# The last expert pair's down product by column halves, and residual rows added by TensorE, in a two-layer hybrid trunk

## What is computed

```
def reference(x, ...):
    h = layer_norm(x, ln_in_g, ln_in_b)
    for l in range(DEPTH):                        # DEPTH = 2
        mix = hybrid_mixer(h, w_in[l], ...)       # begins with p = h @ w_in
        h = layer_norm(DEEPNORM_ALPHA * h + mix, ln_mix_g[l], ln_mix_b[l])
        ffn = grouped_moe(h, w_router, router_bias, w_gate[l], w_up[l], w_down[l])
        h = layer_norm(DEEPNORM_ALPHA * h + ffn, ln_ffn_g[l], ln_ffn_b[l])
    return h

def grouped_moe(h, ...):
    ...
    for e in range(N_EXPERTS):                    # 16
        y = (silu(hf @ w_gate[e]) * (hf @ w_up[e])) @ w_down[e]
        out = out + gates[:, e:e + 1] * y
```

## Time and profile before

| | us |
|---|---|
| median of 3 runs | 691.44 |
| lowest and highest of the 3 | 691.26, 691.76 |
| the profiled execution, whole | 691.46 |
| its span, first to last instruction | 689.6 |
| TensorE busy in the span | 658.3 (95%) |
| VectorE busy | 321.0 (47%) |
| last pair's down, layer 0 | 332.87 to 339.96 |
| last pair's down, layer 1 | 667.82 to 674.91 |

### The profile page before, as it was taken

How to read it: one execution, slowest core, us unless ns; L and a number is a source line. 1 busy time by engine, 2 the same in 40 slices (tenths; PEclk the granted TensorE clock), 3 DMA queues, 4 the chain that set the end, 5 groups by cost and what they waited for, 6 DMA issues and landing times.

```text
span 689.6 us, 7631 instructions
## 1 busy us (share of the span) xinstructions
PE 658.3 (95%) x3105; PEld 339.1 (49%) x3105; DVE 321.0 (47%) x614; ACT 166.7 (24%) x324; POOL 71.2 (10%) x67
## 2 busy tenths in 40 slices
PE   8989999999999999998989999989999999999992
PEld 5854587543333553332478557855333436333331
DVE  6898877610321312320589978682220330320327
ACT  3511753231110221101153138424101114101100
POOL 3503100420000000000070040006000000000001
PEclk9999999999999999999999999999999999999997
DMA  8999936099999999999999973335999999999991
GB/s 286 366 390 414 387 124 244 1 360 397 428 431 428 426 429 427 429 423 419 401 382 395 419 314 123 122 123 208 363 420 428 431 426 429 426 428 429 416 407 66
DMA packets 39580, 240.70 MB, mean 349 GB/s; under 512 B 4524, under 2 KB 8948, under 8 KB 24180
## 3 DMA queue, kind: packets, MB, share of 16 engines
q1 hardware_dynamic: 36756, 236.49, 84.4%
q10 hardware_dynamic: 2784, 3.67, 1.5%
HBM read 239.10 MB, written 1.05 MB: 348 GB/s over the span
## 4 chain that ended last, share of the span: by engine, by line
PE 73%; DVE 11%; DMA 10%; ACT 2%; SPq 1%; issue 1%; POOL 0%; DVEq 0%; POOLq 0%; ACTq 0%
PE bank L591 22%; PE bank L624 10%; DMA ring<-in_w_up 8%; PE bank L495 8%; PE bank L509 6%; PE bank L569 5%; PE bank L606 5%; PE bank L660 4%; PE bank L639 4%; DVE mix L1470 4%; PE bank L707 2%; DMA ring<-in_w_in 2%; DVE in_lo L1236 2%; PE bank L614 1%; PE bank L779 1%
## 5 line engine op out<-in xcount | busy, mean ns | idle before, releaser
L591 PE MATMUL bank<-ring,xe 128*64 128x512 f32 x768 | 167.4, 593 | 0.0
L1397 DVE TENSOR_TENSOR area_b<-area_b,bank 128x512 f32<-128x512 f32 x16 | 11.0, 688 | 230.7 <-PE bank L591 166.6
L591 PEld LDWEIGHTS bank<-ring,xe 128*64 128x64 f32 x768 | 54.8, 137 | 108.3 <-issue 107.8
L624 PE MATMUL bank<-ring,area_b 128*64 128x512 f32 x384 | 85.0, 595 | 0.0
L1417 DVE SCALAR_TENSOR_TENSOR y_lo<-bank,slot_gate,y_hi 128x512 fp32r<-128x512 f32 x32 | 24.0, 750 | 87.7 <-ACT y_hi L984 87.7
L1085 POOL TENSOR_TENSOR rstd<-var_eps,half_neg 128x1 f32<-128x1 f32 x18 | 11.8, 661 | 510.1 <-DVE var_eps L1184 510.1
L606 PE MATMUL bank<-ring,xe 128*64 128x512 f32 x256 | 57.0, 595 | 3.4 <-DMA ring<-in_w_up 2.6
L495 PE MATMUL bank<-ring,xT_area 128*128 128x512 f32 x128 | 55.9, 592 | 0.0
L624 PEld LDWEIGHTS bank<-ring,area_b 128*64 128x64 f32 x384 | 26.5, 137 | 50.0 <-issue 50.0
L1470 DVE SCALAR_TENSOR_TENSOR mix<-mix,tapsT 128x256 f32<-128x256 f32 x120 | 49.8, 476 | 0.0
L984 ACT ACTIVATE y_hi<-bank,slot_gate 128x512 fp32r<-128x512 f32 x32 | 22.0, 687 | 98.4 <-PE bank L624 70.7
(11 more groups left out here) (173 smaller groups left out, 857.7 us busy)
## 6 DMA issues: line engine op xcount, KB each, us to landing
ring<-in_w_gate SPq DMA_DIRECT2D x32, 2048.0 KB, 19.9
ring<-in_w_up SPq DMA_DIRECT2D x32, 2048.0 KB, 20.6
ring<-in_w_down SPq DMA_DIRECT2D x32, 2048.0 KB, 20.7
ring<-in_w_in SPq DMA_DIRECT2D x9, 2048.0 KB, 17.9
ring<-in_w_out SPq DMA_DIRECT2D x4, 2048.0 KB, 20.2
ring<-in_w_in SPq DMA_DIRECT2D x2, 1024.0 KB, 7.7
h<-in_x SPq DMA_DIRECT2D x2, 512.0 KB, 4.0
ln_par<-in_ln_mix_g ACTq DMA_DIRECT2D x2, 512.0 KB, 17.0
```

The source lines that it names most:

```text
L591: mm = pe.matmul(bank[2 + m][e * SLOTS:(e + 1) * SLOTS, :], xe[:, k, at + e * SLOTS:at + (e + 1) * SLOTS], w[e][:, k * DE:(k + 1) * DE], s ...
L624: mm = pe.matmul(bank[5 + n][e * SLOTS:(e + 1) * SLOTS, :], hidT[:, k, e * SLOTS:(e + 1) * SLOTS], w[e][:, k * D + n * BANK:k * D + (n + 1 ...
```

## The change

Five edits.

1. In the last pair of each layer, down goes by column halves: all of half 0 (k = 0 to 3), then half 1. It waits for unit 4 and unit 5 at its beginning, and frees unit 4 after k = 1 of half 1. combine parts 0 and 1 stand inside half 1, ahead of k = 2.
2. add_rows: after down, TensorE multiplies the second half of the residual rows with the identity into bank[2] and bank[3], one fp32 matmul of 128x512 for each block, and combine parts 2 and 3 accumulate on it. VectorE's add_back of parts 2 and 3 is gone in this pair. The statistics of these parts are taken from PSUM, and so is the input of the normalisation, which is now two instructions of 512 columns for each block.
3. VectorE takes add_back 0, 1 and sum_stats 0, 1 between y_lo of half 0 and y_lo of half 1.
4. turn_input transposes half 0 of block 0, half 0 of block 1, half 1 of block 0, half 1 of block 1. ScalarE scales the eight chunks of block 0, VectorE the eight of block 1, and the first slab's products go through the chunks 0 to 7 and wait for both engines at each.
5. KEEP_TURN is 10 where it was 18.

The branch for an expert with more than 64 tokens gets two copies ahead and two behind; with these inputs it isn't entered (the trace has one pass of 8 pairs for each layer).

```diff
-KEEP_START, KEEP_MIX, KEEP_ROUTER, KEEP_SLOTS, KEEP_TURN = 18, 6, 18, 6, 18
+KEEP_START, KEEP_MIX, KEEP_ROUTER, KEEP_SLOTS, KEEP_TURN = 18, 6, 18, 6, 10
...
+            def turn_input(l):
+                for half in range(2):
+                    for b in range(TB):
+                        pe.wait_ge(norm_ready, 2 * TB * l + b + 1)
+                        for c in range(4):
+                            mm = pe.transpose(bank[2 * b + half][:, c * P:(c + 1) * P], normal[:, b, 4 * half + c::KC], ident)
+                        mm.then_inc(tr_pe, 1)
...
+                    if ps.main and j == pairs - 1:
+                        w = [landed_unit(PAIR_UNITS * j + 4 + u).rearrange("p (e c n) -> p e c n", e=2, c=2)
+                             for u in range(2)]
+                        for n in range(2):
+                            for k in range(FC):
+                                if n and k == 2:
+                                    combine(j, (0, 1))
+                                for e in range(2):
+                                    mm = pe.matmul(bank[5 + n][e * SLOTS:(e + 1) * SLOTS, :],
+                                                   hidT[:, k, e * SLOTS:(e + 1) * SLOTS],
+                                                   w[k // 2][:, e, k % 2, n * BANK:(n + 1) * BANK],
+                                                   start=k == 0, stop=k == FC - 1)
+                                if n and k % 2:
+                                    mm.then_inc(ps.used, 1)
+                            if n == 0:
+                                mm.then_inc(s["down_half"], 1)
+                        return
...
+                def add_rows(j):
+                    added(j - 1, 4)
+                    for b in range(TB):
+                        pe.matmul(bank[LAST_COMB_BANKS[2 + b]][:, :], ident, acc[:, b, BANK:D], start=True, stop=False)
...
-                combine(pairs - 1, range(4))
+                if ps.main:
+                    add_rows(pairs - 1)
+                    combine(pairs - 1, (2, 3))
+                else:
+                    combine(pairs - 1, range(4))
...
-                        c = n // 2 + 4 * (n % 2)
+                    for c in range(KC):
                         if k == 2:
-                            pe.wait_ge((tr_act, tr_dve)[n % 2], TR * l + 4 * (TB - 1) + n // 2 + 1)
+                            pe.wait_ge(tr_act, TR * l + c + 1)
+                            pe.wait_ge(tr_dve, TR * l + c + 1)
...
                         if ps.main and j == pairs - 1 and n == 0:
-                            add_back(j, (0,))
+                            add_back(j, (0, 1))
+                            sum_stats(j, (0, 1))
                 if ps.main:
-                    add_back(pairs - 1, (1,))
-                    sum_stats(pairs - 1, (0,))
-                    add_back(pairs - 1, (2,))
-                    sum_stats(pairs - 1, (1, 2))
-                    add_back(pairs - 1, (3,))
-                    sum_stats(pairs - 1, (3,))
+                    for b in range(TB):
+                        nth("comb", pairs - 1, 3 + b, 4)
+                        dve.bn_stats(stats[:, b, 1, :], bank[LAST_COMB_BANKS[2 + b]][:, :]).then_inc(s["stats"], 1)
...
-                        norm_center(norm[b], acc[:, b, :], b)
+                        dve.wait_ge(ln_rstd, norm[b] + 1)
+                        for n in range(2):
+                            ins = dve.tensor_scalar(normal[:, b, n * BANK:(n + 1) * BANK], rows[b][n], mv[:, b, 0:1],
+                                                    rstd[:, norm[b]:norm[b] + 1], ALU.subtract, ALU.mult)
+                        ins.then_inc(norm_ready, 1)
```

More of the change, by code:

```diff
@@ L655, in combine @@
                         if banks[k] == COMB_BANKS[k] and k >= 2:
-                            nth("added", j, k - 1, 4)
+                            added(j, k - 1)
                         elif k < 2 and j:
-                            nth("added", j - 1, k + 3, 4)
+                            added(j - 1, k + 3)
+                        rows_in_bank = ps.main and j == pairs - 1 and n == 1
                         for part in (y_hi, y_lo):
                             mm = pe.matmul(bank[banks[k]][:, :], back[:, b, :], part[:, n * BANK:(n + 1) * BANK],
-                                           start=part is y_hi, stop=part is y_lo)
+                                           start=part is y_hi and not rows_in_bank, stop=part is y_lo)
                         mm.then_inc(s["comb"], 1)
@@ L693, in layer @@
                 u0 = l * LAYER_UNITS
-                for b in range(TB):
-                    pe.wait_ge(norm_ready, 2 * TB * l + b + 1)
-                    turn(normal, b)
+                turn_input(l)
                 w = unit_at(u0).rearrange("p (c n) -> p c n", c=KC)
@@ L1213, in scaled_columns @@
             def scaled_columns(stage, norm):
-                for b in range(TB):
-                    dve.wait_ge(tr_pe, 4 * stage + 2 * b + 2)
-                    for c in range(4):
-                        dve.tensor_scalar(xT[:, 4 + c, b * P:(b + 1) * P], bank[2 * b + 1][:, c * P:(c + 1) * P],
-                                          col_par[:, norm, 0, 4 + c:5 + c], col_par[:, norm, 1, 4 + c:5 + c],
+                for half in range(2):
+                    dve.wait_ge(tr_pe, 4 * stage + 2 * half + 2)
+                    for i in range(4):
+                        c = 4 * half + i
+                        dve.tensor_scalar(xT[:, c, P:2 * P], bank[2 + half][:, i * P:(i + 1) * P],
+                                          col_par[:, norm, 0, c:c + 1], col_par[:, norm, 1, c:c + 1],
                                           ALU.mult, ALU.add).then_inc(tr_dve, 1)
@@ L1377, in add_back @@
                         nth("comb", j, k + 1, 4)
-                        banks = LAST_COMB_BANKS if ps.main and j == pairs - 1 else COMB_BANKS
                         a = acc[:, b, n * BANK:(n + 1) * BANK]
-                        dve.tensor_tensor(a, a, bank[banks[k]][:, :], ALU.add).then_inc(s["added"], 1)
+                        dve.tensor_tensor(a, a, bank[COMB_BANKS[k]][:, :], ALU.add).then_inc(s["added"], 1)
                 def sum_stats(j, parts):
@@ L1544, in _ @@
                 with dve.If(n > SLOTS):
+                    for b in range(TB):
+                        dve.tensor_copy(acc[:, b, BANK:D], bank[LAST_COMB_BANKS[2 + b]][:, :]).then_inc(more.s["stats"], 1)
+                    dve.wait_ge(more.s["stats"], TB)
                     with dve.Fori(0, ROUNDS - 1) as rnd:
@@ L1550, in _ @@
                             experts(l, more, GROUP, rnd, it)
+                    for b in range(TB):
+                        dve.tensor_copy(bank[LAST_COMB_BANKS[2 + b]][:, :], acc[:, b, BANK:D]).then_inc(more.s["stats"], 1)
+                    dve.wait_ge(more.s["stats"], 4 * (ROUNDS - 1) * ITERS + 2 * TB)
                 dve.wait_ge(main.s["stats"], 4 * (l + 1))
                 norm = [norm_variance(b, 2) for b in range(TB)]
+                rows = [(acc[:, b, 0:BANK], bank[LAST_COMB_BANKS[2 + b]][:, :]) for b in range(TB)]
```

43 lines of the change are left out of this document (22 added, 21 removed).

## The result

The changed kernel takes 701.48 us, median of 4 runs (698.88 to 704.08), beside 691.60 for the kernel before (691.26 to 692.07). The ratio is 1.0138, with a 95% interval of 1.0112 to 1.0163. The forecast was 695.8, from 694.3 to 698.3: right in its sign, too small by more than half of the loss. The scatter is new too: 5.2 us between the fastest and the slowest execution, where the kernel before has 0.8.

A forecast was written before the change was run, and what follows sets the result against it. TensorE's path was taken as the bound, with unit 5's landing setting down's start. Layer 0: 4.5 - 2.5 + 0.4 = +2.4; layer 1: 4.4 - 2.5 + 0.15 = +2.0; 691.4 + 4.4 = 695.8 us, range 694.3 to 698.3.

The forecast's parts named there:

- What bounds it: Last pair's down: TensorE's path counts, 95% busy; unit 5's weights land at 336.3 and 671.2, hidden behind unit 4's records.
- Part 1: Down by column halves: waits of 3.41 and 3.35 us for unit 5, combine inside 1.1; +4.5 and +4.4 us.
- Part 2: Tail after down: last statistics 3.8 us after down's end where it was 6.34; 2.5 us won in each layer.
- Part 3: Turn to layer 1: VectorE starts its chunks 1.1 us later, costing +0.4 us (-0.1 to +0.7); KEEP_TURN costs nothing.
- Part 4: Last norm: two instructions in halves in place of one of 1024, twice; +0.15 us for the extra starts.
- The sum: Whole kernel: +2.4 us in layer 0 and +2.0 in layer 1, 691.4 + 4.4 = 695.8 us, 0.6% slower.
- Rival (b): Waits ahead of down: TensorE's clock falls, 2.3 us lost each; one fall 698.1 us (12%), two 700.4 (5%).
- (a): Ahead of down: unit 5 landed long before, no wait; 3.4 us fall away in each layer, 689.0 us; 5%.
- (c): Behind the wait: statistics of half 1 overlap better or the turn gives 0.5 back; 692.8 to 694.4 us; 6%.
- (d): Combine inside down: y_lo of half 0 comes late, TensorE stands still up to 0.3 us in each layer; within forecast's range.

The follow-up runs named there:

- unit-by-unit kernels: Changed kernel with the last pair's down unit by unit and both y_lo ahead of VectorE's additions: 691.44 us; the second also with KEEP_TURN 18: 690.28 us.
- two filled ones: Changed kernel with 14 unread matmuls in the wait ahead of the last pair's down: 697.59 us; the second also with KEEP_TURN 18: 697.13 us.
- two unfilled ones: Changed kernel measured a second time, 701.37 us, and the changed kernel with KEEP_TURN 18, 702.22 us; neither has unread matmuls in the wait ahead of down.
- the turn alone: Kernel before with only the new turn_input order, one engine scaling each block, KEEP_TURN 18: 692.16 us, ratio 0.9996.
- the filled kernel: Changed kernel with 14 unread matmuls put into the wait ahead of the last pair's down: 697.59 us, ratio 1.0074.
- the changed kernel run again: Changed kernel, nothing altered, measured a second time beside other kernels on one chip: 701.37 us, ratio 1.0121.
- the wait-alone kernel: Kernel before with only a wait for units 4 and 5 added ahead of the last pair's down: 703.37 us, ratio 1.0155.
- the KEEP_TURN kernel: Changed kernel with KEEP_TURN back at 18 where it was 10: 702.22 us.
- the half wait: Changed kernel, but half 0 of the last down starts on unit 4 and waits for unit 5 at k = 2: 693.97 us, ratio 1.0021.

## Why the prediction was wrong, step by step

**What bounds it: right.** The landing of the last unit sets the start of down. The wait alone costs more than the whole change, and where down goes unit by unit there is no such wait.

**Part 1: right.** The waits were 3.44 and 3.37 us (forecast 3.41 and 3.35); the four matmuls inside down 1.1 (1.1); y_lo of half 0 was there in time (ready at 343.63, used from 343.73).

**Part 2: right.** add_rows 1.65 to the next start (1.72 forecast), and 3.77 from down to the last statistics (3.8). Here the change does gain, 2.5 us a layer.

**Part 3: right in its chain and size, wrong in a sentence.** The turn came out at +0.33 (forecast +0.4). The four pieces of the normalisation took the 2.45 us of the chain above (2.4 forecast), 0.55 each from SBUF and 0.80 from PSUM, each overlapping the next by some 0.1. But "KEEP_TURN costs nothing either way" isn't borne out. It looked only at whether the transposes would have to wait for the ten matmuls, and not at the clock, which fell at the turn in 3 of 5 profiled executions with ten and in 0 of 7 with eighteen. What that costs is less sure. Eighteen took 1.2 us less between the two unit-by-unit kernels and 0.5 less between the two filled ones, but 0.9 more between the two unfilled ones; no pair is clear of its intervals.

**Part 4: not settled by medians.** Its 0.15 us is less than any median here can tell. In the two profiled executions the chain of waits takes 6.13 us from the end of the last statistics to its end (688.52 to 694.65), where it was 5.88 (681.26 to 687.14): 0.25 more.

**The sum: right to 0.3 us** once the clock is held: 4.65 measured (3.5 to 5.3), 4.4 forecast. That it comes so near is partly luck with such an interval. Its bounds, added up as listed, give 694.5 to 697.2, not 694.4 to 697.0. In the profiled execution of 698.88, 1.4 us are left over 691.4 + 4.4 + 1.7 = 697.5. Of these 0.4 stood ahead of layer 0's down already (it began at 336.71, not at 336.28, behind a wait of the length forecast), and 0.8 came in layer 1 between the last pair's gate and down. There TensorE was 4.4 us behind the kernel before (transposes at 644.50 and 640.12) until it waited for a unit of w_gate, before and after:

```profile
656.26 3.65 PE L606 MATMUL bank<-ring,xe 128*64 128x512 f32 x16 [0.19 <-DMA ring<-in_w_gate]
```

```profile
661.46 3.65 PE L615 MATMUL bank<-ring,xe 128*64 128x512 f32 x16 [1.00 <-DMA ring<-in_w_gate]
```

From there on it was 5.2 behind. This wait differs from kernel to kernel, 0.62 with the turn alone and none in the filled kernel's profile, so nothing shows that it belongs to the change.

**Rival (b): the step that failed.** The sum put TensorE's clock in the new waits at nothing, and the chances put it at 17%, though the mechanism and its place were named and its price was nearly right. The chance rested on one instance, the end of the kernel, where the clock fell 3.4 us after the last work. From that I took that a pause of 3.4 us ends about when the fall would come, and so mostly escapes it. The runs show otherwise in three ways. In the waits the fall came 2.1 to 4.4 us after the last work, so it can come in the middle of the pause, or when TensorE has been working again for 0.9 us, and the new work doesn't stop it. It came in each of the four profiled executions that had the whole waits unfilled, in 6 of their 8 waits. And it can last 6.8 us, not only 3.4, so a wait with a fall cost 1.4 to 2.7 us of work at half speed. I had taken 2.3 for one, from the start of the kernel. That was a stretch ahead of a rise, and read from the pace of the matmuls (0.43 us each, then 0.2); it says nothing on how long a fall lasts. The medians say the same: 3.8 us between the changed kernel and the filled one is more than two falls of 1.7 in an execution. The Trainium skill, page "TensorE: Matmul & The Clock Gate", section "Why this matters for your kernels", which warns of such gaps between bursts, was the better guide than my single row; the traces bear it out in 6 of 8 waits. Its forecast of two falls, 700.4 by my sum, lies 1.1 under what was measured.

Added up, the 8.9 us by which the changed kernel run again lies over its own kernel before are 4.65 without the clock, 0.5 between the two filled kernels (KEEP_TURN), and 3.7 for the clock in the waits. The first four executions were 9.9 over theirs; with a scatter of 5 us nothing shows where that last 1.0 comes from.

**The other rivals.** (a) is ruled out by the wait-alone kernel. (c) did not happen. (d) did not either; the combine inside down never stood still.

## What to carry to other kernels

A reordering that finishes half of a result sooner pays only if its inputs are there: look at the landing of the last transfer, not at the engine's row, which looks busy just because it does first what has landed. Price a new pause of the matrix engine twice, once for its length and once for the clock, and take the fall as the likely case, not the unlucky one, when the pause comes near the distances between last work and fall that the traces show. One trace gives one such distance; look at several. If a shortened tail lets fillers be cut, cut them last, and by runs: here eight unread matmuls at the turn kept the clock up in every profile, for a gain of 1.2 us in one pair of kernels and 0.5 in another. And the part of the change that truly gained, the statistics and rows taken in PSUM, showed only when the rest had been put back.

## What the runs showed of the hardware

The distance from TensorE's last work to the fall of the clock isn't fixed. In the waits it was 3.5 us in layer 0 of the changed kernel, 4.4 and 4.2 in the same kernel run again, 2.9 in layer 0 with KEEP_TURN 18, and 2.2 and 2.1 in the wait-alone kernel; none came in layer 1 of the first and of the KEEP_TURN kernel, in spite of pauses of 3.37 and 3.36 us. At the end of the kernel, where nothing follows, it was 1.5 us (the turn alone) to 5.0 (the changed kernel run again) in the twelve profiled executions. Each fall inside a kernel lasted 3.4 or 6.8 us by the stretches, whatever TensorE did in it. Pauses of 1.49 and 1.42 us inside down brought none in the one profiled execution that has them. Two short pauses with four transposes between them brought one in three of five: 1.58 and 0.47 us in the unit-by-unit kernel, and 1.1 and 0.46 in the half wait and in the changed kernel run again, while the same 1.1 and 0.47 in its first profile brought none.
